# Inverse of a gated delta-rule chunk: levels 1 to 4 on 32x32 diagonal blocks, transposed factor by VectorE

## The reference, cut to what matters

```python
lmat = jnp.where(strict, jnp.einsum('nbhid,nbhjd->nbhij', kb, kc) * decay, 0.0)
eye = jnp.eye(C, dtype=q.dtype)
rhs = jnp.concatenate([kb * jnp.exp(gc)[..., None], vc * bc[..., None]], axis=-1)
sol = lax.linalg.triangular_solve(eye + lmat, rhs, left_side=True, lower=True, unit_diagonal=True)
```

## Time and profile before

| | |
|---|---|
| median of 3 runs | 3641.97 us (3639.04 to 3642.24) |
| profiled execution | 3635.77 us |
| its span, first to last instruction | 3634.1 us |
| PE busy | 3350.6 us (92%) |
| DVE busy | 2024.5 us (56%) |
| ACT busy | 756.3 us (21%) |
| mean granted clock of TensorE | 0.958 of full |

### The profile page before, as it was taken

One profiled execution on the slowest core, in us unless ns is written; L12 is line 12 of the kernel. 1 busy time (PEld: TensorE's weight loads), 2 busy tenths in 40 slices (PEclk: granted clock), 3 DMA queues, 4 the chain that ended last, 5 costly groups with the idle time before them and its releaser, 6 DMA issues.

```text
span 3634.1 us, 63994 instructions
## 1 busy us (share of the span) xinstructions
PE 3350.6 (92%) x27323; PEld 3162.3 (87%) x27323; DVE 2024.5 (56%) x4339; ACT 756.3 (21%) x1577; POOL 859.0 (24%) x775
## 2 busy tenths in 40 slices
PE   6989898989998999988999999995599899999998
PEld 4878787979797888878999999994499799999997
DVE  5556666575756666667867767636512433333334
ACT  3323232323232423222000110112200300000001
POOL 2102120202020202112333333322223233333331
PEclk8999999999999999999999999996699899999999
DMA  2111111111111111110122222226611011111111
GB/s 91 55 48 49 54 50 60 41 54 56 51 50 43 60 42 61 48 37 30 49 79 72 79 75 83 77 72 205 178 41 47 24 48 47 49 47 47 48 48 60
DMA packets 111305, 223.12 MB, mean 61 GB/s; under 512 B 24880, under 2 KB 59184, under 8 KB 110000
## 3 DMA queue, kind: packets, MB, share of 16 engines
q1 hardware_dynamic: 82400, 177.66, 15.8%
q10 hardware_dynamic: 28624, 41.38, 3.5%
HBM read 177.86 MB, written 41.14 MB: 60 GB/s over the span
## 4 chain that ended last, share of the span: by engine, by line
PE 86%; DVE 8%; DMA 2%; ACT 2%; issue 1%; SPq 1%; POOL 0%; POOLq 0%; DVEq 0%; ACTq 0%
PE ps L218 31%; PE ps L624 15%; PE ps L1340 14%; PE ps L657 7%; PE ps L704 5%; PE ps L234 1%; PE ps L679 1%; PE ps L692 1%; PE ps L651 1%; PE ps L636 1%; PE ps L295 1%; PE ps L729 1%; PE ps L685 1%; PE ps L673 1%; PE ps L642 1%
## 5 line engine op out<-in xcount | busy, mean ns | idle before, releaser
L218 PE MATMUL ps<-hhi,whi 128*128 128x344 f32 x2424 | 778.7, 321 | 19.3 <-DVE hlo L1809 14.7
L218 PE MATMUL ps<-hhi,wlo 128*128 128x344 f32 x2424 | 776.0, 320 | 0.0
L218 PE MATMUL ps<-hlo,whi 128*128 128x344 f32 x2424 | 775.2, 320 | 0.0
L2078 POOL TENSOR_TENSOR wtick<-wtick 128x1 f32<-128x1 f32 x213 | 59.2, 278 | 2571.4 <-PE ps L218 817.4
L2081 POOL TENSOR_TENSOR wlo<-wraw,whi 128x1024 fp32r<-128x1024 f32 x213 | 531.8, 2497 | 17.1
L218 PEld LDWEIGHTS ps<-hhi,whi 128*128 128x128 f32 x2424 | 457.4, 189 | 22.4 <-issue 16.6
L218 PEld LDWEIGHTS ps<-hhi,wlo 128*128 128x128 f32 x2424 | 457.0, 189 | 0.0
L218 PEld LDWEIGHTS ps<-hlo,whi 128*128 128x128 f32 x2424 | 456.4, 188 | 0.1
L624 PE MATMUL ps<-hhi,whi 128*128 128x344 f32 x1152 | 388.3, 337 | 6.6 <-DVE olo L1056 2.7
L624 PE MATMUL ps<-hhi,wlo 128*128 128x344 f32 x1152 | 371.7, 323 | 0.0
L624 PE MATMUL ps<-hlo,whi 128*128 128x344 f32 x1152 | 371.0, 322 | 0.0
(11 more groups left out here) (358 smaller groups left out, 5385.4 us busy)
## 6 DMA issues: line engine op xcount, KB each, us to landing
wraw<-in_w SPq DMA_DIRECT2D x213, 512.0 KB, 3.6
dwork<-keep_rows SPq DMA_DIRECT2D x64, 256.0 KB, 3.7
tab<-keep_tab SPq DMA_DIRECT2D x8, 1088.0 KB, 6.5
S<-in_sin ACTq DMA_DIRECT2D x16, 512.0 KB, 3.8
drw<-keep_del SPq DMA_DIRECT2D x32, 256.0 KB, 3.3
out_sout<-S ACTq DMA_DIRECT2D x16, 512.0 KB, 2.7
keep_u<-hs SPq DMA_DIRECT2D x8, 580.0 KB, 3.4
uu<-keep_u SPq DMA_DIRECT2D x8, 580.0 KB, 7.9
```

What stands on the lines that cost most here:

```text
L218: ins = nc.tensor.matmul(out, w, r[:, kt, blk(n)], start=k == 0, stop=k == 3 * KT - 1)
L2078: G.tensor_tensor(wtick[:, 1:2], wtick[:, 0:1], wtick[:, 0:1], ALU.add)
```

## The change

- Levels 1 to 4 work on the four 32x32 diagonal blocks of each matrix: 16 matmuls of 32x32 for each product (`tiles`), each block in its own row group of PE, with the four matrices j in the PSUM banks 0 to 3.
- There are two products a level in place of three. DVE adds PY to Y (YS), and then transposes Y by 32x32 blocks in SBUF (`V.transpose`, TY). The addition to T, and `first_t` with its copy by ACT, are gone.
- The masks NM of levels 1 to 4 are made at once, in one DVE operation in `first_y`.
- The blocks are kept side by side. ACT moves them: `diagonal` (3 copies, in place of DVE's NTc), `spread_t` (2), `spread_y` (4) and `fifth_y` (2), all in slots 9 and 10. `first_y` waits for `diagonal`.
- Level 5 joins 32x32 blocks within each half: P5 (8 matmuls), T5 (4, the one block of T that level 6 needs), PY5 (8). Level 6 is as before, but P6 now also waits for `fifth_y` on ACT.

Eleven small copies stand between the copy of P5 and that of vT. The diff, cut to its core:

```diff
-        NM, PP = (dwork[:, 0].rearrange("p a b -> p (a b)")[:, k * 4 * H:(k + 1) * 4 * H].rearrange("p (j n) -> p j n", n=H) for k in range(2))
-        TT_, YC = (dwork[:, 1].rearrange("p a b -> p (a b)")[:, k * 4 * H:(k + 1) * 4 * H].rearrange("p (j n) -> p j n", n=H) for k in range(2))
+        def compact(i, k, w):
+            return dwork[:, i].rearrange("p a b -> p (a b)")[:, k:k + 4 * w].rearrange("p (j n) -> p j n", n=w)
+        PP, TY_0, TOP, PP6, TY_1 = compact(0, 0, Z), compact(0, 4 * Z, 2 * Z), compact(1, 0, H), compact(1, 4 * H, H), compact(2, 0, 2 * Z)
+        TY = (TY_0, TY_1)
+        NM = dwork[:, 4].rearrange("p a b -> p (a b)").rearrange("p (l j n) -> p l j n", l=4, n=Z)
...
-            def tiles(banks, col, lhsT, rhs):
-                for half, h, c in TILES:
-                    r = slice(H * half, H * half + H)
-                    ins = nc.tensor.matmul(ps[r, banks[h], col + c * H:col + (c + 1) * H], lhsT(r, 2 * h + c), rhs(r, 2 * h + c), start=True, stop=True)
+            def tiles(col, lhsT, rhs):
+                for d in range(4):
+                    for j in range(4):
+                        r = zone((j + d) % 4)
+                        ins = nc.tensor.matmul(ps[r, LEV[j], col:col + Z], lhsT(r, j), rhs(r, j), start=True, stop=True)
...
+            def fifth_level(i, q):
+                gq = f"{i}.{q}."
+                W = TY[q % 2]
+                slot(i, q, 8)
+                p.after("DVE", gq + "TY4")
...
+                        ins = nc.tensor.matmul(ps[low, LEV[jj], COL_P:COL_P + Z], DEC[q % 2][up, jj, low], W[up, jj, 0:Z], start=True, stop=True)
+                p.go(ins, gq + "P5")
+                slot(i, q, 9)
+                p.after("ACT", gq + "P5")
+                for j in range(4):
+                    ins = nc.tensor.matmul(ps[zone(1), LEV[j], COL_T:COL_T + Z], W[zone(1), j, Z:2 * Z], PP[zone(1), j], start=True, stop=True)
+                p.go(ins, gq + "T5")
...
             def last_level(i, q):
...
+                slot(i, q, 10)
                 p.after("DVE", gq + "T5")
+                p.after("ACT", gq + "Y5")
...
             def levels(i, q):
...
-                    p.go(tiles(LEV_A, COL_P, lambda r, j: NM[r, j], lambda r, j: TT_[r, j]), gq + f"P{l}")
+                    p.after("DVE", gq + f"TY{l - 1}")
+                    p.go(tiles(COL_P, lambda r, j: NM[r, l - 1, j], lambda r, j: W[r, j, 0:Z]), gq + f"P{l}")
                     slot(i, q, 2 * (l - 1) + 1)
                     p.after("ACT", gq + f"P{l}")
-                    p.after("DVE", gq + f"Y{l - 1}")
-                    p.go(tiles(LEV_A, COL_T, lambda r, j: YC[r, j], lambda r, j: PP[r, j]), gq + f"TP{l}")
-                    p.go(tiles(LEV_B, COL_Y, lambda r, j: PP[r, j], lambda r, j: YC[r, j]), gq + f"PY{l}")
+                    p.go(tiles(COL_Y, lambda r, j: PP[r, j], lambda r, j: W[r, j, Z:2 * Z]), gq + f"PY{l}")
...
+            def diagonal(i, q):
+                g = f"{i}.{q}."
+                a.after("DVE", g + "NT")
+                for z in range(1, 4):
+                    a.go(A.activation(DEC[q % 2][zone(z), :, 0:Z], DEC[q % 2][zone(z), :, zone(z)], AF.Copy), g + "NTc")
...
+                if s == 9:
+                    spread_t(i, q)
+                    if q + 1 < NQ:
+                        diagonal(i, q + 1)
+                    spread_y(i, q)
                 if s == 10:
+                    fifth_y(i, q)
...
             def first_y(i, q):
                 g = f"{i}.{q}."
+                W, M = TY[q % 2], DEC[q % 2]
+                v.after("ACT", g + "NTc")
+                v.go(V.tensor_tensor(W[:, :, Z:2 * Z], M[:, :, 0:Z], lev[:, 0].unsqueeze(1).to_broadcast([P, 4, Z]), ALU.mult), g + "Y0a")
...
+                v.go(V.tensor_tensor(NM, M[:, :, 0:Z].unsqueeze(1).to_broadcast([P, 4, 4, Z]), lev[:, 1:5].unsqueeze(2).to_broadcast([P, 4, 4, Z]), ALU.mult), g + "NM")
+                v.after("DVE", g + "Y0")
+                v.go(V.transpose(W[:, :, 0:Z], W[:, :, Z:2 * Z]), g + "TY0")
...
-                        v.after("DVE", gq + f"Y{l - 1}")
-                        if l < 6:
-                            v.after("PE", gq + f"TP{l}")
-                            v.go(V.tensor_tensor(side_by(TT_), both(LEV_A, COL_T), side_by(TT_), ALU.add), gq + f"T{l}")
-                        v.after("PE", gq + f"PY{l}")
                         if l < 5:
-                            v.go(V.tensor_tensor(side_by(YC), both(LEV_B, COL_Y), side_by(YC), ALU.add), gq + f"Y{l}")
+                            v.after("DVE", gq + f"TY{l - 1}")
+                            v.after("PE", gq + f"PY{l}")
+                            v.go(V.tensor_tensor(W[:, :, Z:2 * Z], across(COL_Y, Z), W[:, :, Z:2 * Z], ALU.add), gq + f"YS{l}")
+                            v.after("DVE", gq + f"YS{l}")
+                            v.go(V.transpose(W[:, :, 0:Z], W[:, :, Z:2 * Z]), gq + f"TY{l}")
```

More of the change, by code:

```diff
@@ L555, in build, with zone, across @@
         SLOTS = 12
-        COL_P, COL_T, COL_Y, COL_T0 = 0, P, 0, P
-        TILES = [(half ^ h, h, c) for half in range(2) for c in range(2) for h in range(2)]
+        COL_P, COL_T, COL_Y = 0, Z, 2 * Z
         DENSE = (0, 1, 2, 3, 5, 6, 7)
[L559 to L565, removed]
+        LEV, CB = (0, 1, 2, 3), 4
+        def zone(a_):
+            return slice(Z * a_, Z * a_ + Z)
+        def across(col, w, r=slice(0, P)):
+            return ps[r, 0:4, col:col + w]
         PIECE_SLOTS = ((0, 1, 2, 3, 4, 7, 8, 9), (0, 2, 3, 4, 6, 7), (0, 3, 4, 7, 8), (0, 3, 4, 6, 7))
@@ L766, in last_level @@
                 p.after("ACT", gq + "P6")
-                p.after("DVE", gq + "Y5")
                 b = aside("DVE", gq + "Y6", (i * NQ + q + 1) * SLOTS)
                 for j in range(4):
-                    ins = nc.tensor.matmul(ps[0:H, b, j * H:(j + 1) * H], PP[H:P, j], Y[H:P, j, H:P], start=True, stop=True)
+                    ins = nc.tensor.matmul(ps[0:H, b, j * H:(j + 1) * H], PP6[H:P, j], Y[H:P, j, H:P], start=True, stop=True)
                 p.go(ins, gq + "PY6")
@@ L809, in mix_pe @@
                 gram(i, 0, take)
-                for k, _ in enumerate(dense_steps(i, 5)):
-                    if k == 3:
-                        for b in LEV_B:
-                            use(b, "ACT", f"{i}.0.T0")
-                        first_t(i, 0)
-                for b in LEV_A + LEV_B:
+                for _ in dense_steps(i, 5):
+                    pass
+                for b in LEV:
                     p.after(*held[b])
@@ L818, in mix_pe @@
                     levels(i, q)
-                held[LEV_A[0]] = ("ACT", f"{i}.{NQ - 1}.P6")
-                held[LEV_A[1]] = ("DVE", f"{i}.{NQ - 1}.T5")
-                for b in LEV_B:
-                    held[b] = ("DVE", f"{i}.{NQ - 1}.Y5")
+                for b in LEV:
+                    held[b] = ("ACT", f"{i}.{NQ - 1}.P6")
             e = HQK - 1
@@ L874, in decay, with spread_t, spread_y, fifth_y @@
                 a.go(A.activation(f4(DEC[q % 2]), f4(DEC[q % 2]), AF.Exp), g + "expd")
-            def first_t(i, q):
+            def diagonal(i, q):
                 g = f"{i}.{q}."
-                a.after("PE", g + "T0t")
-                a.go(A.activation(side_by(TT_), both(LEV_B, COL_T0), AF.Copy), g + "T0")
+                a.after("DVE", g + "NT")
+                for z in range(1, 4):
+                    a.go(A.activation(DEC[q % 2][zone(z), :, 0:Z], DEC[q % 2][zone(z), :, zone(z)], AF.Copy), g + "NTc")
+            def spread_t(i, q):
+                g = f"{i}.{q}."
+                a.after("DVE", g + "TY4")
+                for z in range(2):
+                    a.go(A.activation(TOP[zone(z), :, zone(z)], TY[q % 2][zone(z), :, 0:Z], AF.Copy), g + "TOP")
+            def spread_y(i, q):
+                g = f"{i}.{q}."
+                for z in range(4):
+                    a.go(A.activation(YY[q % 2][zone(z), :, zone(z)], TY[q % 2][zone(z), :, Z:2 * Z], AF.Copy), g + "YD")
+            def fifth_y(i, q):
+                g = f"{i}.{q}."
+                a.after("PE", g + "PY5")
+                for z in (0, 2):
+                    a.go(A.activation(YY[q % 2][zone(z), :, zone(z + 1)], across(COL_Y, Z, zone(z)), AF.Copy), g + "Y5")
             def chain(i, q, k):
```

95 lines of the change are left out of this document (40 added, 55 removed).

## The result

The change made the kernel slower: 3666.6 us median against 3641.0 us of before on the same chip, ratio 1.0068, 95% interval [1.0052, 1.0084], where 3593 us had been forecast. A fourth run of it, at a mean granted clock of 0.63, took 4690 us: it counts in the median of four and not in the ratio, and the other three lie between 3662.5 and 3670.4. The profiled execution took 3662.5 us with a span of 3660.7; before's span was 3634.1.

The account below looks back on a forecast made before the run. PE was taken to bind in most places, DVE in a few. Savings of 7.0 us a round over seven rounds, 49 us, took the profiled 3635.8 to 3587, plus 6 for the median: 3593 us, range 3552 to 3672.

Parts of the forecast that it names:

- The sum: Whole kernel: rounds 1 to 7 save 7.0 us each, 49 in all, round 0 nothing; median 3593 us.
- half-clock stretches as many as before: TensorE: a sign that the forecast is right, the number of stretches at half clock unchanged.
- TensorE's clock: Rival: the stall before P6 starts a further low-clock stretch in each quad, 43 us, giving 3636 us; 12 in 100.
- one such stretch more: TensorE, each quad: one added half-clock stretch like the 3.3 us one in quad 2, 32 x 1.35 = 43 us.
- quad 1 stayed at 1.00 before: Argument against the clock falling: quad 1, with a 0.72 us wait and many small tiles, kept the full clock.
- The small pass: PE, levels 1 to 4: a 32x32 tile takes 0.033 us where row groups alternate; bounds 0.0145 and 0.058.
- The rival of the pass: PE: a small pass doesn't shrink below 0.029 us, 118 us over the forecast's sum, 3682 us; 20 in 100.
- YS, transposition and level latency: DVE, each level: addition 0.29 us, transposition 0.29 us, 0.95 us from PY to the next P.
- a: Time mark in quad 1, the last issue of PY4; NT forecast to end at a+3.6, P6 to go at a+5.75.
- ScalarE's copies: ACT, slots 9 and 10: 0.21 us a copy, P6 waiting for 11 copies, PE standing 2.4 us.
- the bound of 0.35: Rival: ACT's copies cost their full 0.35 us without overlap, 42 us in all, 3635 us; 14 in 100.
- The quads: Forecast savings in rounds 1 to 7: quad 1 0.8 us, quad 2 2.0, quad 3 1.5 and 0.6.

Follow-up runs that it names:

- e15: The changed kernel with `diagonal` behind `fifth_y` and the next quad's Gram products ahead of slot 7's recurrence step, no unused matmuls; ratio to before 0.9962.
- e9: The changed kernel with `diagonal` behind `fifth_y`, eight unused 128x344 matmuls before P6, and Gram products ahead of slot 7's recurrence step; ratio to before 0.9875.
- e1: The changed kernel with eight unused 128x344 matmuls ahead of slot 10's v transposes, in front of P6, in every quad; ratio to before 0.9988.
- e2: The changed kernel with ScalarE's three `diagonal` copies for the next quad moved behind the two of `fifth_y`; ratio to before 1.0040.
- e4: The changed kernel with the `diagonal` copies moved behind `fifth_y` and eight unused 128x344 matmuls in front of P6; ratio to before 0.9952.
- e8: The changed kernel with every 32x32 pass of levels 1 to 4 issued twice; ratio to before 1.0281.
- e10: The kernel before the change with eight unused 128x2 matmuls ahead of slot 10's v transposes; ratio to before 1.0020.
- e11: The changed kernel with two unused 128x344 matmuls ahead of each group of 32 passes in levels 1 to 4; ratio to before 1.0218.

## Why the prediction was wrong

The step that failed is TensorE's clock. The sum put it at nothing ("half-clock stretches as many as before"), and the rival *TensorE's clock* priced it at "one such stretch more" a quad, 43 us in all, with 12 in 100. The half clock grew by 307 us up to the mixer's end, 9.6 us a quad, where the rival had one stretch like the 3.3 us of the earlier trace rows.

What a microsecond of it costs can be read in two ways. The first is from pairs that differ by the fill: 31 us for 147 (e15 to e9), 29 for 85 (after to e1) and 32 for 79 (e2 to e4), so 0.21 to 0.41, the fill's own cost included. The second needs no fill. In after itself the interval from quad 0 to quad 1 holds the same work in each of the rounds 1 to 7; it took 21.6 to 22.0 us in the three with at most 1.1 us of half clock in it, and 23.8 to 24.5 in the four with 6.8 to 8.3. Over all 21 intervals of after, each kind taken from its own mean, the slope is 0.31. By 0.21 to 0.41 the 307 us took some 65 to 125 us, and without them the change would have saved 40 to 100 us, an estimate, in which the sum's 49 lies. So the levels' saving is real and was given back by the clock.

The place shows it too. Against the forecast the interval that ends in quad 2 came out 5.2 us long in each of seven rounds, that of quad 3 2.5, the stretch to quad 0 of the next round 3.1, that of quad 1 1.4 short, and round 0 9 long: together the 75 us between the forecast of the span and the span. In quad 2's interval the half clock grew by 13 us on the mean, at 0.31 some 4 of the 5.2.

I had argued that quad 1 stayed at 1.00 before in spite of small tiles; but a group of 32 passes held TensorE for 1.15 us there and for 0.45 now. That this difference brings the clock down isn't shown: e8 held it 0.41 us longer a group and had only 24 us less half clock.

Point by point:

- **The small pass** was mis-sized in the good direction: 0.016 us a tile, near my low bound of 0.0145, as if four row groups overlapped wholly. The 0.033 wasn't the half of 0.058 that the text claims (0.029), which made the sum 0.5 us a quad too long by its own rule. The rival of the pass is refuted: 0.45 us a group, not 1.15. The Trainium skill's rule that start-to-start never drops below about 25 ns ("TensorE: Matmul & The Clock Gate", Wait — 56ns, not 53.3ns?) does not hold across row groups here: 8 ns measured.
- **YS, transposition and level latency** were right: 291 and 312 ns; TY ended 1.0 us after the last pass of PY4 was issued (0.95 forecast). The 311 ns of the Trainium skill ("VectorE: DVE Perf Modes", The three transpose paths), listed for bf16, is what the f32 blocks took. NT ended at a+3.6, as forecast (a is 1161.1 here).
- **ScalarE's copies** were mis-sized in the sum: 0.33 us each in a row, near the bound of 0.35 that I had given 14 in 100. The pair in the earlier trace rows, two copies of 0.365 us with starts 0.265 apart, was no guide to `diagonal`, `spread_y` and `fifth_y`, where each copy starts 0.02 us behind the end of the one before. Why is open: `diagonal` itself starts 0.09 us before `spread_t` ends in 14 quads. So `diagonal` ended at a+4.6, `spread_y` at a+5.95, `fifth_y` at a+6.5 and P6 went at a+6.7, 0.9 late; PE stood 3.11 us, not 2.4. ScalarE's busy time grew by 70 us, not 58; VectorE's fell by 137, not 110. (Its share in the four quads of the earlier trace rows was 68 to 81%, not the 59 to 81 that the prediction read.)
- **The quads.** For the intervals of 25.3, 32.4 and 25.0 us before, which end in quads 1, 2 and 3, I had -0.8, -2.0 and -2.1. Where no half clock fell in the first it was 22.0 us in after, -3.3: more than I had forecast, as the cheaper pass would give. The mean of after is 23.1, 35.6 and 25.4. A round grew by 2.4 us (seven rounds: 17) and round 0, for which I had taken nothing, by 9, with 65 us of half clock in it against 10; together 26 of the 27 us of the span.
- **"Half-clock stretches as many as before"** was the sign to look for, and it told: 71 against 38 in the whole run.

Did the longer wait for the copies bring the clock down, or the emptier levels? The wait has its part. In the mixer of after 51 half-clock stretches begin, 386 us; 19 of them, 130 us, begin between 0.5 us before and 4 us behind the start of a P6. In before it was 2 of 21 (10 us), and in e9, with the fill, 5 of 37 (20 us). But two thirds of after's lie elsewhere, and in e4 and e9, where TensorE stands only 6 us before P6 in all 32 quads, as in before (4), the half clock is still 297 and 242 us against 106. Less array work beside the 64x64 levels didn't bring it down (e10, without a wait of 3 us), and neither small nor wide passes put back into the levels brought it up by much (e8, e11). So how much the levels give to the fall stays open, as does the rest of the half clock in quad 0 and in round 0, which no run lifted at no cost.
